# Triangular inverse of the delta-rule phase: two fp32r projection products behind each level's Z products, eighteen ahead of the first transposes, none behind the head's last

## What is computed

```python
kb = k * beta[..., None]
lower = jnp.where(strict, jnp.einsum('bhnid,bhnjd->bhnij', kb, k) * decay, 0.0)
t_inv = lax.linalg.triangular_solve(eye + lower, eye, left_side=True, lower=True,
                                    unit_diagonal=True)
w = t_inv @ (kb * jnp.exp(gc)[..., None])
u = t_inv @ (v * beta[..., None])
...
v_new = u_n - w_n @ S
o_n = qd_n @ S + qk_n @ v_new
S = S * dec_n[..., None, None] + jnp.swapaxes(kd_n, -1, -2) @ v_new
```

## Time and profile before

| | |
|---|---|
| median of three runs | 1338.55 us (1337.31 to 1342.82) |
| the profiled execution | 1341.28 us, span 1339.6 us |
| TensorE busy | 1238.4 us, 92% of the span |
| VectorE, ScalarE, GpSimd busy | 457.9, 311.3, 398.5 us |
| mean granted TensorE clock | 0.974 |

### The profile page before, as it was taken

How to read it: one execution, slowest core, us unless ns; L and a number is a source line. 1 busy time by engine, 2 the same in 40 slices (tenths; PEclk the granted TensorE clock), 3 DMA queues, 4 the chain that set the end, 5 groups by cost and what they waited for, 6 DMA issues and landing times.

```text
span 1339.6 us, 23794 instructions
## 1 busy us (share of the span) xinstructions
PE 1238.4 (92%) x8545; PEld 778.1 (58%) x8546; DVE 457.9 (34%) x923; ACT 311.3 (23%) x829; POOL 398.5 (30%) x424
## 2 busy tenths in 40 slices
PE   8999999999999989999999999987789979979896
PEld 5587778877774458888558654443344435534442
DVE  3755665556415443323248211111011111101115
ACT  3332333423313442222231111011111011101111
POOL 2545534355504340000000333233223322233321
PEclk9999999999999999999999899988899999989998
DMA  4621112115024223335904599999999998999995
GB/s 129 185 62 55 55 47 70 55 55 172 1 64 122 57 58 96 85 95 188 422 34 141 214 379 402 399 394 397 395 405 396 397 398 347 353 400 397 393 339 197
DMA packets 117965, 296.42 MB, mean 221 GB/s; under 512 B 11976, under 2 KB 81736, under 8 KB 101360
## 3 DMA queue, kind: packets, MB, share of 16 engines
q1 hardware_dynamic: 100384, 267.75, 52.4%
q0 software_dynamic: 15344, 25.12, 7.8%
q10 hardware_dynamic: 2144, 2.22, 0.5%
HBM read 280.93 MB, written 26.51 MB: 230 GB/s over the span
## 4 chain that ended last, share of the span: by engine, by line
PE 35%; DMA 21%; DVE 3%; issue 3%; POOL 1%; POOLq 0%; SPq 0%; ACT 0%; DVEq 0%; ACTq 0%
PE bank L1380 11%; PE bank L1980 10%; DMA sum_rows<-expert_y,row_col 8%; DMA expert_gu<-in_expert_w_gate_up_dram 6%; PE bank L1987 5%; PE bank L1386 4%; DMA sum_rows<-over_y,over_row_col 4%; DMA expert_down<-in_expert_w_down_dram 2%; PE bank L1972 1%; PE bank L2054 1%; PE bank L1408 1%; PE bank L2032 1%; PE bank L1401 1%; DMA gathered_x<-x_rows,tok_col 0%; DVE x_rows L2246 0%
## 5 line engine op out<-in xcount | busy, mean ns | idle before, releaser
L1980 PE MATMUL bank<-expert_gu,gathered_xT 128*64 128x256 f32 x2016 | 250.1, 400 | 31.7 <-DMA expert_gu<-in_expert_w_gate_up_dram 21.7
L1980 PEld LDWEIGHTS bank<-expert_gu,gathered_xT 128*64 128x64 f32 x2016 | 141.3, 138 | 121.8 <-issue 22.3
L2180 DVE SCALAR_TENSOR_TENSOR hidden<-gate,slot_w,bank 128x128 f32<-128x128 f32 x64 | 22.2, 347 | 434.1 <-ACT gate L2138 423.0
L1987 PE MATMUL bank<-expert_down,hiddenT 128*64 128x512 f32 x504 | 126.4, 623 | 18.7 <-issue 18.0
L1877 POOL DMA_INDIRECT sum_rows<-expert_y,row_col x62 | 98.2, 1584 | 47.9 <-POOL row_col L1874 46.3
L486 PE MATMUL bank<-x_high,w_head_low 128*128 128x512 f32 x224 | 93.8, 419 | 0.0
L486 PE MATMUL bank<-x_low,w_head_high 128*128 128x512 f32 x224 | 93.4, 417 | 0.0
L486 PE MATMUL bank<-x_high,w_head_high 128*128 128x512 f32 x224 | 93.4, 417 | 0.0
L1874 POOL COPY row_col<-row_idx 128x1 int32 (+1 forms) x62 | 12.0, 194 | 258.3 <-DMA sum_rows<-expert_y,row_col 136.9
L2149 ACT COPY expert_y<-bank 128x512 f32<-128x512 f32 x63 | 36.9, 585 | 180.2 <-PE bank L1987 104.3
L2138 ACT ACTIVATE gate<-bank 128x128 f32<-128x128 f32 x64 | 17.9, 279 | 247.9 <-PE bank L1980 247.9
(11 more groups left out here) (388 smaller groups left out, 2233.5 us busy)
## 6 DMA issues: line engine op xcount, KB each, us to landing
expert_gu<-in_expert_w_gate_up_dram SPq DMA_DIRECT2D x63, 2048.0 KB
expert_down<-in_expert_w_down_dram SPq DMA_DIRECT2D x63, 1024.0 KB
w_head<-in_w_in_dram SPq DMA_DIRECT2D x32, 512.0 KB, 3.9
w_tile<-in_w_in_dram SPq DMA_DIRECT2D x14, 512.0 KB, 4.2
x_rows<-in_x_dram SPq DMA_DIRECT2D x8, 512.0 KB, 6.5
sum_rows<-zero_rows SPq DMA_DIRECT2D x2, 2048.0 KB, 12.1
w_tile<-in_w_branch_a_dram SPq DMA_DIRECT2D x7, 512.0 KB, 5.7
w_pair<-in_w_in_dram SPq DMA_DIRECT2D x6, 512.0 KB, 5.5
```

Source lines behind the costliest of these rows:

```text
L1980: mm = nc.tensor.matmul(bank[parts[a], 0:2 * P], x[:, c, part], halves[:, a, :, :], start=(c == 0), stop=(c == KC - 1))
L1987: mm = nc.tensor.matmul(bank[parts[a], :], hidden_t[:, c * BLK:(c + 1) * BLK], dn[:, c, a * (D // 2):(a + 1) * (D // 2)], start=(c == 0), ...
```

## The change

Three numbers change in how many products are issued where; the list, its order, the total of 96 (144) and all else stay.

```diff
-                fill(20)
+                fill(18)
...
                         mm.then_inc(tok_psum[g], 1)
...
                             mm = along(ps[3], n, p, y_of, x_of)
                     mm.then_inc(zt_psum[l], 1)
-                    fill(1)
+                    fill(2)
```

## The result

Twenty runs of each kernel, on several occasions:

| | median | lowest to highest |
|---|---|---|
| before | 1344.35 us | 1337.31 to 1351.40 |
| after | 1337.37 us | 1332.33 to 1345.13 |
| after / before | 0.995 | 0.9932 to 0.9967 (95%) |

The account below looks back on a forecast made before the run. TensorE was taken to bound the delta phase. Gains of 5.2, 3.2 and 0.7 us less 0.8 make 8.3 us, which from a median of 1338.55 gives 1330.3 us, range 1327.5 to 1334.5.

Parts of the forecast that it names:

- What bounds the kernel: Delta phase: TensorE sets the pace, busy 41.6 of every 42.4 us, so a microsecond saved there is one of the whole.
- The second product behind Z: Gap between Z and Y, five levels, eight heads: an added product costs 0.02 us instead of 0.23, 0.8 us in all.
- The Trainium skill's rule on weight loads: Small loads before Y: if pulled ahead, last spacing 0.23 us, not 0.33, and the 0.8 us cost nothing; measured 0.33 speaks against.
- The two products ahead of the first transposes: Removing them saves 0.46 us a head, 3.2 us over seven heads; nothing in head 0, where TensorE already waits for XT.
- The three products behind line 648: Crossing to the next head's line 556: removal saves 0.74 us, 5.2 us for seven crossings, plus 0.7 in the last head.
- Is the data there earlier too: Squares to XT: the chain moves 0.48 us earlier, leaving XT ready 0.1 us ahead of TensorE's need, wait costed at nothing.
- What moves with the group borders: Taps, loads and GpSimd's split released by the 24th, 48th and 96th products shift in time; claimed to cost nothing.
- XT as the bound: Rival at the inverse products: XT stays late, 0.38 us in seven heads, gain 5.6 us, time 1332.9 us; chance 0.12.
- The gain swallowed later: Rival in the experts' stage: its end is tied to something not starting earlier, time stays near 1338.5 us; chance 0.08.
- Not hidden: Rival behind Z: the second product costs up to 0.33 us in 40 gaps, 4.1 us slower, 1342.7 us; chance 0.06.
- The time and its range: Whole kernel: 8.3 us off the earlier median of 1338.55 gives 1330.3 us, range 1327.5 to 1334.5 us.
- Faster, same, slower: Whole time, border at half a per cent, 1331.9 us: faster 0.66, within 0.30, slower by more 0.04.

Follow-up runs that it names:

- gap0: Kernel before with no product behind Z instead of one and 25 instead of 20 ahead of the first transposes; delta phase 358.25 us, head to head 43.32 us.
- gap3: Kernel before with three products behind Z, 18 ahead of the first transposes, 7 ahead of line 648, none behind it; delta phase 349.85 us, head to head 42.12 us.
- front15: Kernel before with two products behind Z and 15 instead of 20 ahead of the first transposes; delta phase 351.1 us, head to head 41.85 us.
- cut kernels: Mix and experts left out: from the kernel before 500.25 and 500.52 us, from the changed kernel 491.21 and 491.06, from tail_ahead 500.17.
- before_again: Kernel before, unchanged, traced a second time; delta phase 349.82 us, span 1338.6 us.
- tail_ahead: Kernel before with only the three products behind line 648 moved ahead of it (15 instead of 12); delta phase 349.73 us, span 1337.8 us.

## Why the prediction was right or wrong

**What bounds the kernel.** Right. TensorE sets the delta phase's pace; 8.3 us taken out of its program shortened the phase by 8.45 and 8.27 us.

**The second product behind Z.** Right, and cheaper than forecast. Each level grows by at most 0.02 us; from X's transposes to line 608 it is 15.46 us instead of 15.42, so 0.3 us for eight heads and not 0.8. gap0 and gap3 show the limits: with none or one the level takes 2.77 us, with two 2.78 or 2.79, with three 3.01 to 3.03.

**The Trainium skill's rule on weight loads** ("TensorE: Matmul & The Clock Gate", "Step-by-step: what each phase is for") would have the small loads pulled ahead if their row groups don't conflict or they go to the spare weight buffer. From the second product to Y it is 0.32 and 0.33 us (144.03 to 144.35, 146.81 to 147.14), not 0.23, as it was in the earlier trace rows. The trace doesn't show small loads pulled ahead here, and whether they meet either condition no run tells.

**The two products ahead of the first transposes.** Right: 7.82 us from line 556 to X's transposes became 7.35. In head 0 the wait grew from 0.76 to 1.19 us, and nothing was gained, as said.

**The three products behind line 648.** Right: 1.14 us became 0.43, a saving of 0.71 where 0.74 was forecast.

**Is the data there earlier too.** Right in its outcome, wrong in its size. XT's end moved by 0.62 us with respect to line 648 (8.03 us behind it before, 7.41 after) and not by 0.48. The step: I let the squares start 0.02 us behind the end of the silus, but they start at 133.45, while the last silu is still recorded until 133.54. So the slack is 0.27 us (140.06 less 139.69 and 0.10) and not 0.1.

**What moves with the group borders.** Costs nothing, as forecast. front15 shows what it costs when a border crosses a place of VectorE's program: 0.4 us a head.

**The rivals.** XT as the bound: not in the changed kernel, real in front15, 0.31 us a head. The gain swallowed later: not so, as the cut kernels keep all of it up to the mix; behind that, one stretch at the lower clock took 1.5 us of the first trace's gain. before_again has it too, so it doesn't need the changed order; both traces of the changed kernel have it, though, and two traces don't tell chance from a tie. Not hidden: fallen, by gap0.

**The time and its range.** This is where the prediction failed. The step is "The profiled execution took 1341.28 us ... it lies 2.7 us above the median of 1338.55, from which the same 8.3 us give 1330.3 us", together with the 1.5 us of spread in the range. Three runs with a spread of 5.5 us don't place a median to 1.5 us: twenty gave 1344.35, with 14 us from the fastest to the slowest, and nine each on two later occasions, on two different chips, gave 1344.14 and 1346.75. The mechanism and the gain were right; the term that was mis-sized is the level, by 5.8 us, and the spread around it. With that level the same 8.3 us give 1336.05, 1.3 us from the 1337.37 measured. The cut kernels show that nearly all of the spread is made in the mix and the experts. The traces, which all lie between 1331 and 1344 us of span, have differences of up to 4.1 us in the experts' stretch alone. Two of them there (before, then gap0; columns as in the earlier trace rows):

```profile
744.70:1305.40 560.70, 496.30 (x3273) 246.16 (x3272) 76.14 (x155) 72.84 (x212) 171.63 (x219) 0.95 0.99 380
...
751.10:1309.10 558.00, 495.25 (x3272) 246.40 (x3272) 76.11 (x155) 72.94 (x212) 171.86 (x219) 0.95 0.99 382
```

The DMA engines are busy 0.99 of this stretch in all eight traces. Its length goes with the time that TensorE has half clock in it: 51.2 us in the three traces of 558.0 to 559.4, 54.6 in those of 559.3 and 560.3, 58.0 in those of 560.7 and 561.8, 61.4 in that of 562.1. Whether the clock makes the length, or waits that make the length also let the clock fall, no run here separates, so the cause of the spread stays open. The earlier trace rows had its two signs, 334 GB/s from memory and a granted clock of 0.96, and I read them only for a rival. The lower bound also has a slip: 1330.3 less 0.8, 0.3 and 1.5 is 1327.7 and not 1327.5; it changes nothing.

**Faster, same, slower.** The measured 0.5% lies on the border that I had drawn. The phase's gain is 0.62% of 1344; the whole's interval, 0.33% to 0.68%, doesn't tell it from there.

## What to carry to other kernels

If an engine sets the pace and stands idle in gaps that another engine's latency makes, work moved into the gaps gains what it cost where it stood, less what the gaps grow: here five products of 0.23 us less 0.04 us, 1.11 us a head, where 42.16 less 41.04, 1.12 us, was measured. The idle time of a gap only says how much fits: 0.31 us took one product of 0.23 and not two. Measure the gap as distance between starts against the same distance where nothing waits. When work is moved along a list, follow what the list's borders release, and every wait that the moved work had covered, not only the next one. Price the change in the stage that it touches, but take the level and the range of the whole from the spread of its noisiest stage: a few runs of this kernel, whose last phase keeps the DMA engines busy 0.99 of a stretch of 560 us, fixed neither.

## What the runs showed that I had not expected

- A stop of 1.97 us at a barrier was followed by 3.4 us at half the clock in three of eight traces and by none in the other five, on unchanged code. The kernel before is on both sides. The stop of 2.3 us at the barrier ahead of it was followed by one in six of the eight. One such stretch cost 0.5, 1.5 or 1.6 us, by its place.
- ScalarE's next operation starts 0.09 us ahead of the recorded end of the one before, when nothing holds it; in a chain with 0.1 us of slack that was as much as the slack.
- The setup phase ended 0.2 to 1.0 us sooner in the changed kernel's traces than in those of before, though its code is the same: first transposes at 49.3 and 49.6 against 50.2 and 50.3 us, and 48.35 and 48.55 against 48.93 and 48.79 with the last phase left out. tail_ahead, which differs from before in one count, has 49.4 whole and 48.8 cut, and gap0, gap3 and front15 have 49.3 to 49.5. The traces don't say why.
